# Splitting the last two plain fp32 weight units of an expert pair, with ScalarE and GpSimd

## The chip, the cores and the metric

One core of one Trainium2 chip runs the whole program. The metric is the device time of one execution in microseconds (us). A weight here is fp32; the kernel multiplies at fp32 accuracy by splitting a weight into a rounded part (type fp32r) and the rest, and adding two products.

## What is computed

One encoder layer over 16 meta tokens and 256 tokens of width 2048: a mixer (latent attention and retention), then a mixture of 32 experts in 4 groups, top 2 inside the top group. The change lies in the experts:

```python
def ffn(args):
    xb, e = args
    return (jax.nn.silu(xb @ w1[e]) * (xb @ w3[e])) @ w2[e]
```

w1 and w3 are 2048x512 for each expert, w2 is 512x2048, all float32: 12 MB an expert, 384 MB in all. Every expert's weights are read once a round.

## The kernel before, in words

**Units and pairs.** The mixer comes first (up to about 1163 us of the span). The experts' stage, from about 1206 us, goes over 16 pairs of experts (PAIRS). A pair has 24 weight units of 1 MB, [128 partitions x 2048] fp32, numbered x = 0 to 23: four each of w1, w3, w1 (the second expert), w2 (the first), w3 (the second), and w2 of the second, which is worked on four units into the next pair. A step k = x + 4 counts from there, so k = 0 is unit 20 of the pair before, and unit 22 is worked on at k = 2 of the next pair. Unit 10 is at k = 14.

**One unit's way.** SyncE loads it into one of 8 slots of raw2 (RING2), as soon as TensorE has finished unit x - 8. ScalarE rounds it into one of 4 slots of wh2 (`hi`, line 512), which it may do when TensorE has finished unit x - 4 (HELD). VectorE takes the difference, wl2 = raw2 - wh2, in place of raw2 (`lo`, line 623). TensorE (`unit`) multiplies with both: lines 869 and 870, four matmuls of 512 columns each, then counts the unit in s_used2. The profile names these tiles raw, wh and wl.

**The two plain units.** XR = (10, 22): these two units of a pair are neither rounded nor subtracted. TensorE reads raw2 as fp32 (line 866), in four matmuls that the profile records as eight passes.

**Order.** Each engine's program is written out by hand. In a step ScalarE first does copies that are due (L525: the finished products ab), then `hi(x + 4)`, then sigmoid (L529), the scaled output yall (L535) and the copies of gathered tokens (L517, at k = 4, 6, 8, 10, 16, 18, 20, 22). VectorE does `lo(x + 4)`, then `hidden` (L731 to L741, at k = 0 and 12), `output_rest` (L748, at k = 7 and 19) and `select` (L723, L724, at k = 9). TensorE does the unit, then `mix` (L891, L894, at k = 0 and 12: it waits for `select` and for the copies of ab), then the gathers (L850). GpSimd has only the scatters of finished rows (L479), one for each expert: parity 0 behind k = 19, parity 1 behind k = 7 of the next pair. The stage is one round here (the loop `more` is not entered).

```python
XR = (10, 22)
X_SPLIT = [sum(y not in XR for y in range(x)) for x in range(25)]
raw2 = place("raw2", [P, RING2, U], 0)
wl2 = place("wl2", [P, RING2, U], 0, F32R)
wh2 = place("wh2", [P, HELD, U], 65536, F32R)
```

Of the kernel before, what the change touches and what calls it, by code (L numbers as in the profile page):

```python
# [5 lines left out]
F32 = mybir.dt.float32  # L6
# [3 lines left out]
ALU = mybir.AluOpType  # L10
ACT = mybir.ActivationFunctionType
# [38 lines left out]
HELD = 4  # L50
# [41 lines left out]
def moe_trunk(nc, ins, out):  # L92
# [12 lines left out]
    def sem(name):  # L105
        return ctx.enter_context(nc.semaphore(name))

    with ctx:
# [50 lines left out]
        st = place("st", [P, 2, 3 * P], R0 + 6144)  # L159
# [113 lines left out]
        XR = (10, 22)  # L273
# [5 lines left out]
# [3 lines that stand above are left out]
# [49 lines left out]
        s_h1 = sem("s_h1")  # L331
# [12 lines left out]
        s_raw2 = [sem(f"s_raw2_{i}") for i in range(RING2)]  # L344
        s_wh2 = sem("s_wh2")
        s_wl2 = sem("s_wl2")
        s_used2 = sem("s_used2")
        s_ac = sem("s_ac")
        s_bc = sem("s_bc")
# [28 lines left out]
        def slot2(x):  # L378
            return (x + 4) % RING2

        def landed2(turn, x):

            return 16 * (24 // RING2 * turn + (x + 4) // RING2 + (slot2(x) >= 4))
# [90 lines left out]
        def pool_experts(pool):  # L474
            def scatter(filled, par):

                pool.wait_ge(s_h1, 1)
                pool.wait_ge(s_ye[par], filled)
                pool.indirect_dma_start(yscr[:, :], bass.IndirectOffsetOnAxis(dest[0:SLOTS, par:par + 1], 0),  # L479
                                        yall[0:SLOTS, par, :], None, bounds_check=SCRATCH_ROWS - 1,  # L480
                                        oob_is_err=False).then_inc(s_scat[par], 16)

            def pairs(first, end):
                with pool.Fori(first, end) as p:
                    scatter(p, 0)
                    scatter(p, 1)

            pairs(1, PAIRS + 1)
            pool.wait_ge(s_nx, 1)
            more = pool.value_load(nxi[0:1, 0:1], min_val=0, max_val=ROUNDS - 1)  # L490
            with pool.If(more > 0):
                pairs(PAIRS + 1, PAIRS * (more + 1) + 1)
            for par in range(2):
                pool.wait_ge(s_scat[par], 16 * PAIRS * (more + 1))
            nc.gpsimd.tensor_tensor(marks[:, 5:6], half[:, 0:1], half[:, 0:1], ALU.mult).then_inc(s_all, 1)

        def scalar_experts(act):

            act.wait_ge(s_wused, N_UNITS)
            for b in range(KD):  # L500
                act.wait_ge(s_h1t, b + 1)
                nc.scalar.activation(h1t[:, b, :], ps[:, b % 8, 0:SEQ], ACT.Copy).then_inc(s_h1tc, 1)

            def hi(turn, x):
                if x % 24 in XR:
                    return
                act.wait_ge(s_raw2[slot2(x)], landed2(turn, x))
                if isinstance(turn, int) and 24 * turn + x < HELD:
                    act.wait_ge(s_wused, N_UNITS)
                else:  # L510
                    done(act, turn, x - HELD)
                nc.scalar.activation(wh2[:, x % HELD, :], raw2[:, slot2(x), :], ACT.Copy).then_inc(s_wh2, 1)  # L512

            def gathered(g, par, q):

                act.wait_ge(s_gt, 8 * g + q + 1)
                nc.scalar.activation(xg[:, par, 2 * q:2 * q + 2, :, :],  # L517
                                     ps[:, 7 - q % 2, :].rearrange("p (k a c) -> p k a c", k=2, a=2),
                                     ACT.Copy).then_inc(s_xg, 1)

            def copy_up(turn, x, j, v):

                done(act, turn, x)
                need(act, s_hm, j)
                nc.scalar.activation(ab[:, v, :], ps[:, v, :], ACT.Copy).then_inc((s_ac, s_bc)[v], 1)  # L525

            def sigmoid(j):
                act.wait_ge(s_hm, j + 1)
                nc.scalar.activation(sg[:, :], ps[:, 6, 0:4 * SLOTS], ACT.Sigmoid).then_inc(s_sg, 1)  # L529

            def outputs(turn, x, j, par, before_):

                done(act, turn, x)
                need(act, s_scat[par], 16 * before_)
                nc.scalar.activation(yall[0:SLOTS, par, :].rearrange("p (b c) -> p b c", b=4), ps[0:SLOTS, 2:6, :],  # L535
                                     ACT.Copy, scale=wsc[0:SLOTS, par:par + 1]).then_inc(s_yc, 1)

            def pair(turn, par, first=False):
                for x in body(first):
                    k = step(x, first)  # L540
                    if k == 11:
                        copy_up(turn, x, 2 * turn, 1)
                    if k == 23:
                        copy_up(turn, x, 2 * turn + 1, 1)
                    hi(turn, x + HELD)
                    if k == 0 and not first:
                        sigmoid(2 * turn - 1)
                    if k == 3:
                        copy_up(turn, x, 2 * turn, 0)
                    if k == 7 and not first:  # L550
                        outputs(turn, x, 2 * turn - 1, 1, turn - 1)
                    if k == 12:
                        sigmoid(2 * turn)
                    if k == 15:
                        copy_up(turn, x, 2 * turn + 1, 0)
                    if k == 19:
                        outputs(turn, x, 2 * turn, 0, turn)
                    for q in range(8):
                        if k == (G_FIRST if first else G_AT)[q]:
                            gathered(turn + 1, 1 - par, q)  # L560

            def one_round(turn, ready=0):
                for x in range(ready, HELD):
                    hi(turn, x)
                pair(turn, 0, first=True)
                pair(turn + 1, 1)
                with act.Fori(1, PAIRS // 2) as i:
                    pair(turn + 2 * i, 0)
                    pair(turn + 2 * i + 1, 1)
                last = turn + PAIRS - 1  # L570
                sigmoid(2 * last + 1)
                outputs(last, 23, 2 * last + 1, 1, last)

            for x in range(HELD):
                hi(0, x)
            for n in range(2):
                act.wait_ge(s_r1, n + 1)
                dst = eg if n == 0 else ex
                nc.scalar.activation(dst[:, :, :], dst[:, :, :], ACT.Exp).then_inc(s_r2, 1)
            for q in range(8):  # L580
                gathered(0, 0, q)
            one_round(0, ready=HELD)
            act.wait_ge(s_nx, 1)
            more = act.value_load(nxi[0:1, 0:1], min_val=0, max_val=ROUNDS - 1)
            with act.If(more > 0):
                with act.Fori(0, more) as r:
                    one_round(PAIRS * (r + 1))
# [228 lines left out]
        def tensor_experts(pe):  # L816

            pe.wait_ge(s_h1, 1)
            for b in range(KD):
                need(pe, s_h1tc, b - 7)  # L820
                for t in range(TT):
                    m = nc.tensor.transpose(ps[:, b % 8, P * t:P * (t + 1)], mrg[:, t, P * b:P * (b + 1)], ident[:, :])
# [3 lines left out]
            for t in range(TT):  # L826
                for b in range(KD):
                    m = nc.tensor.matmul(ps[:, 6 + t, 0:N_GROUPS + N_EXP], h1t[:, b, P * t:P * (t + 1)], wr[:, b, :],
                                         start=b == 0, stop=b == KD - 1)
# [24 lines left out]

            def unit(turn, x, pairs_, start, stop):

                raw = x % 24 in XR
                if raw:
                    pe.wait_ge(s_raw2[slot2(x)], landed2(turn, x))
                else:  # L860
                    pe.wait_ge(s_wl2, split_units(turn, x) + 1)
                one = len({id(a[0]) for a in pairs_}) == 1
                for i, (o, s, c) in enumerate(pairs_):
                    st, sp_ = (start and (i == 0 or not one)), (stop and (i == 3 or not one))
                    if raw:
                        m = nc.tensor.matmul(o, s.bitcast(F32), raw2[:, slot2(x), c:c + 512], start=st, stop=sp_,  # L866
                                             skip_group_check=True)
                    else:
                        nc.tensor.matmul(o, s, wh2[:, x % HELD, c:c + 512], start=st, stop=False, skip_group_check=True)  # L869
                        m = nc.tensor.matmul(o, s, wl2[:, slot2(x), c:c + 512], start=False, stop=sp_,  # L870
                                             skip_group_check=True)
                m.then_inc(s_used2, 1)

            def up(turn, x, u, v, par, a):
# [1081 lines left out]
```

## Time and profile before

| | |
|---|---|
| median of 3 runs | 2248.09 us (2244.63 to 2248.26) |
| the profiled execution | 2248.71 us |
| its span | 2246.6 us |
| mean granted TensorE clock | 0.969 |
| busy: TensorE / VectorE / ScalarE / GpSimd | 2124.5 / 1573.4 / 1238.8 / 107.8 us |
| HBM read / written | 590.90 / 18.87 MB |

The profile is one execution. In its views each row is a group of instructions or a stretch of time; "busy" is the union of the times in which an engine worked, an arrow `<-` with a name behind it tells what ended an engine's idle time. Matmul ends are modelled, so the distance of two starts tells more than a matmul's length. PE is TensorE, PEld its weight load, DVE VectorE, ACT ScalarE, POOL GpSimd, SP SyncE.

### The profile page before, as it was taken

What the parts mean: (1) busy time and instruction counts of PE and PEld (TensorE: products, weight loads), DVE (VectorE), ACT (ScalarE), POOL (GpSimd) and SP (SyncE); (2) the same over time, 40 slices, a digit from 0 to 9 for tenths busy, and PEclk for the clock granted to TensorE, in tenths of its full rate; (3) what the DMA queues carried; (4) which work ended last, traced back from release to release, by engine and by line L of the source; (5) the groups of instructions that cost most, each with busy time, mean ns of one, the idle gap of its engine ahead of it and who ended that gap; (6) DMA issues with size and microseconds to landing.
All of it is one profiled execution on the core that took longest, in us unless ns stands there. A gap on an engine that the chain in (4) does not pass through costs nothing.

```text
span 2246.6 us, 30190 instructions
## 1 busy us (share of the span) xinstructions
PE 2124.5 (95%) x11513; PEld 1773.6 (79%) x11513; DVE 1573.4 (70%) x1348; ACT 1238.8 (55%) x1007; POOL 107.8 (5%) x76
## 2 busy tenths in 40 slices
PE   6999999999999999999978999999999999999991
PEld 5998777899998987887867777778777778777770
DVE  6545444453546365544466999989999999999986
ACT  3434443333232323333334888878887878888870
POOL 1000000000000000001000000000000000000001
PEclk9999999999999999999977999999999999999995
DMA  5554334655454544555544999999999999999973
GB/s 186 150 142 159 95 112 150 209 180 177 148 171 145 167 150 145 196 188 192 173 168 171 410 412 418 412 397 420 420 420 410 415 417 413 417 404 421 407 313 152
DMA packets 161974, 598.23 MB, mean 266 GB/s; under 512 B 20016, under 2 KB 28320, under 8 KB 110544
## 3 DMA queue, kind: packets, MB, share of 16 engines
q1 hardware_dynamic: 158224, 589.60, 69.2%
q0 software_dynamic: 3680, 7.64, 1.0%
q8 instruction: 50, 0.82, 0.1%
q14 instruction: 20, 0.16, 0.0%
HBM read 590.90 MB, written 18.87 MB: 271 GB/s over the span
## 4 chain that ended last, share of the span: by engine, by line
PE 74%; DVE 13%; issue 9%; ACT 2%; DMA 1%; POOL 1%; DVEq 0%; SPq 0%; POOLq 0%; ACTq 0%
PE ps L1551 20%; PE ps L1535 14%; PE ps L869 9%; DVE wl L623 9%; PE ps L870 9%; PE ps L866 5%; PE ps L850 3%; PE ps L891 3%; PE ps L1642 2%; PE ps L1622 2%; ACT wh L512 1%; PE ps L1609 1%; DVE yall L748 1%; PE ps L1663 1%; DMA yrow<-yscr 1%
## 5 line engine op out<-in xcount | busy, mean ns | idle before, releaser
L623 DVE TENSOR_TENSOR wl<-raw,wh 128x2048 fp32r<-128x2048 f32 x352 | 786.6, 2286 | 58.7 <-ACT wh L512 57.4
L512 ACT ACTIVATE wh<-raw 128x2048 fp32r<-128x2048 f32 x352 | 664.8, 1912 | 122.2 <-PE ps L870 71.9
L1198 DVE TENSOR_TENSOR wl<-raw,wh 128x2048 fp32r<-128x2048 f32 (+1 forms) x169 | 382.2, 2264 | 310.2 <-ACT wh L1031 310.2
L1031 ACT ACTIVATE wh<-raw 128x2048 fp32r<-128x2048 f32 (+1 forms) x169 | 319.9, 1896 | 463.4 <-DMA raw<-in_w_in_dram 283.6
L869 PE MATMUL ps<-wh,xg 128*128 128x512 f32 x900 | 382.4, 425 | 0.8 <-issue 0.7
L870 PE MATMUL ps<-wl,xg 128*128 128x512 f32 x900 | 359.4, 399 | 0.0
L1535 PE MATMUL ps<-hth,wh 128*128 128x272 f32 (+1 forms) x896 | 260.0, 290 | 5.0 <-DVE wl L1198 3.6
L1535 PE MATMUL ps<-htl,wh 128*128 128x272 f32 (+1 forms) x896 | 256.9, 287 | 0.0
L1535 PE MATMUL ps<-hth,wl 128*128 128x272 f32 (+1 forms) x896 | 256.8, 287 | 0.0
L869 PEld LDWEIGHTS ps<-wh,xg 128*128 128x128 f32 x900 | 173.4, 193 | 52.4 <-DVE wl L623 9.7
L869 PE MATMUL ps<-wh,hx 128*128 128x512 f32 x508 | 204.6, 403 | 3.4 <-DVE hx L741 3.4
L870 PEld LDWEIGHTS ps<-wl,xg 128*128 128x128 f32 x900 | 173.6, 193 | 40.6 <-issue 7.4
L870 PE MATMUL ps<-wl,hx 128*128 128x512 f32 x508 | 200.1, 394 | 0.0
L1535 PEld LDWEIGHTS ps<-hth,wh 128*128 128x128 f32 x896 | 169.5, 189 | 8.0 <-issue 3.5
L1535 PEld LDWEIGHTS ps<-htl,wh 128*128 128x128 f32 x896 | 169.4, 189 | 0.3
L1535 PEld LDWEIGHTS ps<-hth,wl 128*128 128x128 f32 x896 | 169.1, 189 | 0.0
L1551 PE MATMUL ps<-wh,hth 128*128 128x512 f32 x384 | 154.6, 403 | 0.0
L1551 PE MATMUL ps<-wh,htl 128*128 128x512 f32 x384 | 151.0, 393 | 0.0
L1551 PE MATMUL ps<-wl,hth 128*128 128x512 f32 x384 | 150.9, 393 | 0.0
L479 POOL DMA_INDIRECT yscr<-yall,dest x32 | 73.3, 2292 | 980.1 <-DVE yall L748 980.1
L869 PEld LDWEIGHTS ps<-wh,hx 128*128 128x128 f32 x508 | 96.4, 190 | 23.1 <-DVE hx L741 3.5
L866 PE MATMUL ps<-raw,xg 128*128 128x512 f32 x248 | 113.3, 600 | 0.0
(315 smaller groups left out, 3105.0 us busy)
## 6 DMA issues: line engine op xcount, KB each, us to landing
raw<-in_w_dram SPq DMA_DIRECT2D x384, 1024.0 KB, 8.1
raw<-in_w_in_dram SPq DMA_DIRECT2D x104, 1024.0 KB, 5.1
raw<-in_w_pa_dram SPq DMA_DIRECT2D x16, 1024.0 KB, 5.1
raw<-in_w_pb_dram SPq DMA_DIRECT2D x16, 1024.0 KB, 5.1
raw<-in_w_out_dram SPq DMA_DIRECT2D x16, 1024.0 KB, 5.1
raw<-in_w_ukv_dram SPq DMA_DIRECT2D x8, 1024.0 KB, 5.4
yrow<-yscr SPq DMA_DIRECT2D x4, 1024.0 KB, 9.8
raw<-in_w_uq_dram SPq DMA_DIRECT2D x8, 384.0 KB, 3.6
```

Of the source, the lines that this page charges most:

```text
L479: pool.indirect_dma_start(yscr[:, :], bass.IndirectOffsetOnAxis(dest[0:SLOTS, par:par + 1], 0), yall[0:SLOTS, par, :], None, bounds_check= ...
L512: nc.scalar.activation(wh2[:, x % HELD, :], raw2[:, slot2(x), :], ACT.Copy).then_inc(s_wh2, 1)
L623: nc.vector.tensor_tensor(wl2[:, slot2(x), :], raw2[:, slot2(x), :], wh2[:, x % HELD, :].bitcast(F32), ALU.subtract).then_inc(s_wl2, 1)
L850: m = nc.tensor.matmul(bank[:, b, :, h, :], src[:, t, 2 * q + b, :], pg[:, t, :].rearrange("p (a s) -> p a s", a=2), start=t == 0, stop=t ...
L866: m = nc.tensor.matmul(o, s.bitcast(F32), raw2[:, slot2(x), c:c + 512], start=st, stop=sp_, skip_group_check=True)
L869: nc.tensor.matmul(o, s, wh2[:, x % HELD, c:c + 512], start=st, stop=False, skip_group_check=True)
L870: m = nc.tensor.matmul(o, s, wl2[:, slot2(x), c:c + 512], start=False, stop=sp_, skip_group_check=True)
L891: nc.tensor.matmul(ps[:, 6, c:c + SLOTS], ab[:, v, P * f:P * (f + 1)], fold[:, :], start=True, stop=True, skip_group_check=True)
L1031: nc.scalar.activation(wh[:, n % RING1, 0:c], raw1[:, n % RING1, 0:c], ACT.Copy).then_inc(s_wh, 1)
L1198: nc.vector.tensor_tensor(wl[:, n % RING1, 0:c], raw1[:, n % RING1, 0:c], wh[:, n % RING1, 0:c].bitcast(F32), ALU.subtract).then_inc(s_wl, 1)
L1535: m = nc.tensor.matmul(ps[:, bank, col:col + width], w[:, n % RING1, c:c + P], s[:, 4 * u + k, c0:c0 + width], start=opens and u == 0 and ...
L1551: m = nc.tensor.matmul(ps[:, bank + t, :], s[:, 4 * u + k, c:c + P], w[:, n % RING1, 512 * k:512 * (k + 1)], start=u == 0 and k == 0 and j ...
```

## The change

Units 10 and 22 go the same way as the others up to the difference. ScalarE rounds them too, in their turn of the order. Their difference is made by GpSimd (`residue`), in place over raw2, ahead of the scatter of the same parity. Two semaphores each (s_hx for rounded, s_lx for subtracted) take the place of s_wh2 and s_wl2 for these units, so that the counts of the other 22 stay. TensorE waits for s_lx in place of the load, and has one form of unit. VectorE's program is unchanged.

```diff
+        s_hx = [sem(f"s_hx{i}") for i in range(len(XR))]
+        s_lx = [sem(f"s_lx{i}") for i in range(len(XR))]
...
+            def residue(filled, i):
+
+                x = XR[i]
+                pool.wait_ge(s_h1, 1)
+                pool.wait_ge(s_hx[i], filled)
+                nc.gpsimd.tensor_tensor(wl2[:, slot2(x), :], raw2[:, slot2(x), :], wh2[:, x % HELD, :].bitcast(F32),
+                                        ALU.subtract).then_inc(s_lx[i], 1)
+
             def pairs(first, end):
                 with pool.Fori(first, end) as p:
+                    residue(p, 0)
                     scatter(p, 0)
+                    residue(p, 1)
                     scatter(p, 1)
...
             def hi(turn, x):
-                if x % 24 in XR:
-                    return
+                made = s_hx[XR.index(x % 24)] if x % 24 in XR else s_wh2
...
-                nc.scalar.activation(wh2[:, x % HELD, :], raw2[:, slot2(x), :], ACT.Copy).then_inc(s_wh2, 1)
+                nc.scalar.activation(wh2[:, x % HELD, :], raw2[:, slot2(x), :], ACT.Copy).then_inc(made, 1)
...
             def unit(turn, x, pairs_, start, stop):
 
-                raw = x % 24 in XR
-                if raw:
-                    pe.wait_ge(s_raw2[slot2(x)], landed2(turn, x))
+                if x % 24 in XR:
+                    pe.wait_ge(s_lx[XR.index(x % 24)], turn + x // 24 + 1)
...
-                    if raw:
-                        m = nc.tensor.matmul(o, s.bitcast(F32), raw2[:, slot2(x), c:c + 512], start=st, stop=sp_,
-                                             skip_group_check=True)
-                    else:
-                        nc.tensor.matmul(o, s, wh2[:, x % HELD, c:c + 512], start=st, stop=False, skip_group_check=True)
-                        m = nc.tensor.matmul(o, s, wl2[:, slot2(x), c:c + 512], start=False, stop=sp_,
-                                             skip_group_check=True)
+                    nc.tensor.matmul(o, s, wh2[:, x % HELD, c:c + 512], start=st, stop=False, skip_group_check=True)
+                    m = nc.tensor.matmul(o, s, wl2[:, slot2(x), c:c + 512], start=False, stop=sp_,
+                                         skip_group_check=True)
```

## Rows read from the trace of the kernel before

**Rows 1.** The page: GB/s that the DMA engines moved, span in 40 slices.
```profile
GB/s 186 150 142 159 95 112 150 209 180 177 148 171 145 167 150 145 196 188 192 173 168 171 410 412 418 412 397 420 420 420 410 415 417 413 417 404 421 407 313 152
```

**Rows 2.** Timeline of GpSimd: start, duration, instruction, idle time before and who ended it.
```profile
1255.11 2.27 POOL L479 DMA_INDIRECT yscr<-yall,dest  x1 [103.53 <-DVE yall L748]
...
1654.91 2.26 POOL L479 DMA_INDIRECT yscr<-yall,dest  x1 [27.44 <-DVE yall L748]
1685.79 2.25 POOL L479 DMA_INDIRECT yscr<-yall,dest  x1 [28.63 <-DVE yall L748]
...
2176.85 2.25 POOL L479 DMA_INDIRECT yscr<-yall,dest  x1 [28.63 <-DVE yall L748]
```

**Rows 3.** Two pairs: PE, PEld, DVE, ACT, POOL busy; clock, DMA share, GB/s.
```profile
1625.22:1685.79 60.57, 59.61 (x297) 47.45 (x297) 57.90 (x40) 50.93 (x39) 4.50 (x3) 1.00 1.01 421
1685.79:1747.99 62.20, 61.22 (x297) 48.71 (x297) 57.89 (x40) 50.91 (x39) 4.50 (x2) 0.97 1.01 412
```

**Rows 4.** The same view, at a fall of the granted clock in another pair.
```profile
1415.00:1420.00 5.00, 5.00 (x12) 3.13 (x12) 3.12 (x8) 1.97 (x2) 0.00 (x0) 0.67 1.01 410
```

**Rows 5.** Pair from 1625.22: tile raw (idle until, landing), then the DMA view.
```profile
  ACT wh L512: 2.3, 4
...
DMA to landing us min/median/max: 6.5/8.2/10.2
...
GB/s 411 427 427 427 417 417 427 422 417 422 427 433 417 411 433 411 422 422 427 433 406 422 433 422 417 422 417 433 400 417 406 417 411 422 422 411 433 422 433 422
DMA packets 3615, 25.50 MB, mean 421 GB/s; under 512 B 503, under 2 KB 503, under 8 KB 503
```

**Rows 6.** Groups by line from 1400 to 2100 us: busy, mean ns, idle before.
```profile
L623 DVE TENSOR_TENSOR wl<-raw,wh 128x2048 fp32r<-128x2048 f32 x251 | 560.8, 2286 | 39.6 <-ACT wh L512 38.8
L512 ACT ACTIVATE wh<-raw 128x2048 fp32r<-128x2048 f32 x250 | 472.2, 1912 | 89.5 <-PE ps L870 52.4 <-PE ps L866 36.5 <-DMA raw<-in_w_dram 0.5
```

**Rows 7.** Waits from 1400 to 2100 us: us in total, times, longest.
```profile
PE ps L891 <- DVE wdc L724: 11.6, 12, 1.0
```

**Rows 8.** Timeline of TensorE: mix, a plain unit (x = 10), a split one; unit 22 last.
```profile
1659.51 1.99 PE L891 MATMUL ps<-fold,ab 128*128 128x64 f32 x16 [0.96 <-DVE wdc L724]
...
1663.67 3.59 PE L866 MATMUL ps<-raw,xg 128*128 128x512 f32 x8
1666.70 0.79 PE L869 MATMUL ps<-wh,xg 128*128 128x512 f32 x1
1667.33 0.40 PE L870 MATMUL ps<-wl,xg 128*128 128x512 f32 x1
1667.56 0.39 PE L869 MATMUL ps<-wh,xg 128*128 128x512 f32 x1
...
1693.37 3.60 PE L866 MATMUL ps<-raw,xg 128*128 128x512 f32 x8
```

**Rows 9.** Timeline of ScalarE around unit 10, and the roundings before unit 22.
```profile
1653.37 1.91 ACT L512 ACTIVATE wh<-raw 128x2048 fp32r<-128x2048 f32 x1
1656.58 0.60 ACT L525 ACTIVATE ab<-ps 128x512 f32<-128x512 f32 x1 [0.82 <-PE ps L870]
1657.07 3.70 ACT L512 ACTIVATE wh<-raw 128x2048 fp32r<-128x2048 f32 x2
...
1663.87 1.91 ACT L512 ACTIVATE wh<-raw 128x2048 fp32r<-128x2048 f32 x1 [1.54 <-PE ps L870]
...
1684.23 1.91 ACT L512 ACTIVATE wh<-raw 128x2048 fp32r<-128x2048 f32 x1
```

**Rows 10.** Groups by line: the smallest tensor_tensor of GpSimd and of VectorE.
```profile
L495 POOL TENSOR_TENSOR marks<-half 128x1 f32<-128x1 f32 x1 | 0.4, 408 | 2.3 <-DMA yscr<-yall,dest 2.3
...
L735 DVE TENSOR_TENSOR dest<-ps,beyond 128x1 uint32<-128x1 f32 x32 | 4.7, 148 | 0.0
```

**Rows 11.** Timeline of VectorE around the mix of 1659.51.
```profile
1654.10 4.49 DVE L623 TENSOR_TENSOR wl<-raw,wh 128x2048 fp32r<-128x2048 f32 x2
1658.52 0.68 DVE L723 TENSOR_TENSOR pd<-slots,rk__144 128x512 f32<-128x512 f32 x1
```

## The prediction, made before the changed kernel had run

> **What bounds the kernel now.** I read the page first. The slices [rows 1] show the experts' stage from about 1206 us on: the DMA engines move 400 to 420 GB/s there, twice what they do before it. The 16 pairs of experts repeat, and GpSimd's scatters mark them [rows 2]: one scatter of each pair starts at 1255.11 us and the same one of the last pair at 2176.85 us, 15 pairs in 921.7 us, so 61.45 us a pair. The pairs are of two kinds. The one from 1625.22 takes 60.57 us at a granted clock of 1.00, the next takes 62.20 us at 0.97 [rows 3]. In the slow kind TensorE ran for a while at the lower of its levels, 1.2 instead of 2.4 GHz; such a fall lies at 1415 to 1420 us too, with a mean of 0.67 and TensorE busy all the time [rows 4].
>
> None of three resources is idle enough to be set aside, as the busy times of the clean pair show. In its 60.57 us TensorE (PE) is busy 59.61 us, VectorE (DVE) 57.90 us, so that it is idle 2.67 us; ScalarE (ACT) is busy 50.93 us, GpSimd (POOL) 4.50 us, and the DMA engines report a share of 1.01 [rows 3]. A load lands 8.2 us after its issue (median) while 24 of them share 60.57 us, one each 2.52 us, so three are in flight all the time, at 421 GB/s [rows 5]. The waits say the rest: ScalarE waits for TensorE to free a slot of wh (52.4 and 36.5 us in 700 us), VectorE for ScalarE (38.8 us), hardly anybody for a DMA (0.5 us) [rows 6], and TensorE waits now and then for VectorE, 12 times for the select alone [rows 7]. So two resources are nearly used up, VectorE with 2.67 us to spare in a pair and the DMA engines with about nothing, and TensorE's order of work ties them together.
>
> **What the change removes.** On TensorE a plain unit is eight passes: the next unit starts 3.03 us after the first pass at 1663.67, and its second product 0.63 us later, where 0.23 us is the usual step, so the unit occupies 3.03 + 0.40 = 3.43 us [rows 8]. A split unit is eight matmuls 0.23 us apart (1667.33 to 1667.56), 1.84 us. Two units a pair: 2 x 1.6 = 3.2 us of TensorE's time go. That alone buys little. The waits of ScalarE for L866 (36.5 us in the 700 us, or 3.2 us a pair) and part of VectorE's for L512 go with it, but what is late next is the DMA: it moves 25.50 MB a pair at 421 GB/s [rows 5], and its best slices are 427 to 433. At 427 GB/s a pair would be 59.7 us. So the most that the removal can give is 61.45 - 60.57 = 0.9 us a pair if only the slow kind of pair goes, or 1.75 us if the DMA also reaches 427: 14 to 28 us over 16 pairs.
>
> **What it adds on ScalarE.** Two roundings a pair at 1.91 us [rows 6], 3.8 us; busy time goes from 50.93 to 54.7 us of 60.57. They fall into the holes: hi(10) would start at 1655.2, when the rounding of 1653.37 ends, and end at 1657.1; a copy of gathered tokens and the one of 1656.58, half a microsecond each, then come before the roundings of 1657.07, which start at about 1658.0, 0.9 us late. ScalarE has 1.54 us idle ahead of 1663.87 to make it good [rows 9]. VectorE's difference of 1659.19 starts perhaps 0.7 us late. I cost it at nothing, covered by such idle time at each of the two places; without that cover it is up to 0.9 us a place, 1.8 us a pair, 29 us in all.
>
> **What it adds on GpSimd.** Two tensor_tensor of 128x2048 fp32 a pair, in place over raw. No row shows GpSimd reading a tile of that size. From below I bound it by the same form on VectorE, 2286 ns [rows 6]. From above: on the smallest form (128x1) GpSimd takes 408 ns and VectorE 148 ns [rows 10], 2.76 times, and 2.76 x 2.286 = 6.3 us. That factor is mostly fixed cost, the lower end assumes an engine built for such work; I take the middle, D = 4.3 us. The Trainium skill, "GPSIMD Engine Reference", section 3.1, gives 4497 ns for a GpSimd tensor_tensor add of 2048 fp32 elements; no run here shows it, and with it the sum below would end at 2342 us.
>
> Does TensorE wait for it? For x = 10, hi(10) ends at 1657.1 and TensorE wants the unit at 1663.67: 6.5 us of cover. For x = 22, GpSimd is free from its scatter at 1688.04, hi(22) ends at about 1688.0 (behind the rounding of 1684.23, ahead of the gathered copy), and TensorE wants it at 1693.37: 5.3 us of cover [rows 2, 8, 9]. With D = 4.3 both fit. In GpSimd's queue the scatter of parity 0 stands behind residue(10), which is over 24 us before it is due, and the scatter of parity 1 behind residue(22), due some 22 us later. GpSimd idles 27 to 29 us between scatters [rows 2], so nobody waits there.
>
> **What it does to VectorE** decides. Both engines then read whole tiles of raw and wh and write wl at the same time, VectorE without a pause. No row shows the two together on tiles. The nearest is the scatter at 1654.91, 2.26 us long, beside the two differences of 1654.10, which still take 4.49 us together [rows 2, 11]; but there GpSimd writes descriptors and reads no tile. So the loss s of VectorE per residue lies between 0 and D (a gain is excluded: VectorE's instructions are the same in number and size). VectorE has no queue to spare: a pair would take the larger of 60.57 us and 57.90 + 2s + 0.37 us, where 0.37 is the idle time of a clean pair that isn't a wait for L512 (2.67 - 2.3) [rows 3, 5]. That passes today's 61.45 us at s = 1.6 us. Of the interval from 0 to 4.3 us, 63% lies above that. I take the upper end, s = D: two differences on VectorE itself never overlap (1654.10: two in 4.49 us [rows 11]), and an instruction of the same kind, on the same two tiles, that must go through the same memory counts for me as if it stood in that queue, at its longer duration. The place can be seen: residue(10) would take over at 1658.5, between the second difference and the select of L723 [rows 11]; the select, the mix of 1659.51 behind it [rows 8] and all later differences move back by D. The Trainium skill, "SBUF — State Buffer", section "Who interferes with whom", says that a VectorE instruction with two SBUF inputs and a GpSimd instruction that reads SBUF exclude each other, and that the later one blocks for the whole of the earlier. It speaks against this change; no row here shows it, and by it s is D less what falls beside VectorE's PSUM forms.
>
> **The sum.** 57.90 + 2 x 4.3 + 0.37 = 66.9 us a pair against 61.45: +5.4 us, 16 pairs: +87 us. The profiled execution took 2248.7 us (its span of 2246.6 and 2.1 around it), 0.6 us above the median of the three runs, so I add to it: 2248.7 + 87 = 2335 us. With D = 2.29 it is +1.4 a pair, 2272 us; with D = 6.3 it is +9.4, 2400 us. TensorE saves 3.2 us a pair that nobody needs, and the DMA engines fall to 25.50 / 66.9 = 381 GB/s.
>
> **Rivals.**
> A. No interference (s near 0), faster. For it: the untouched 4.49 us beside the scatter. Then VectorE has its 2.67 us, the plain units' delay is gone, the pairs of 62.20 us become 60.57 or less, and the DMA ends it: 2248.7 - 14 = 2235 us, down to 2220 if 427 GB/s hold. It decides up to s = 1.15 us ((60.57 - 58.27) / 2). Against it: TensorE would stand idle oftener, and the falls of its clock may go on.
> B. Partial interference, s from 1.15 to 3 us: 60.6 to 64.3 us a pair, 2235 to 2294 us. For it: GpSimd needs more time per element than VectorE, so it can't use the memory all the time.
> C. GpSimd slower than its cover without harming VectorE: at D = 6.3 the x = 22 unit is 1.0 us late (6.3 - 5.3), and ScalarE's 1.8 us come on top: 16 x 2.8 = +45 less the 14 gained, 2280 us at the most, about 2250 if only one of them acts. Against it: TensorE is ahead of the other two elsewhere.
> D. The units aren't cheaper on TensorE, that is, the change doesn't do what it says. It would matter in A only (2249 us); the rows of all other split units speak against it.
>
> **How the numbers follow.** The forecast (s = D, 2300 to 2400 us) has 0.50, A 0.24, B 0.18, C and D 0.08. Within 0.2% of before (about what a measurement of this kernel can tell from no change, here 2244 to 2253 us) lie the part of B with s from 1.45 to 1.75 us (0.03) and half of C and D (0.04), together 0.07. Faster are A and the part of B with s under 1.45 us, 0.27; the rest, 0.66, is slower. The range starts at 2233 us, which takes in the main value of A, and ends at 2365 us, D = 5.2 us (57.90 + 10.4 + 0.37 = 68.7, 16 x 7.2 = 116); above and below it I leave 0.15. The slow cases' own range is 2270 to 2365.
>
> **What would show it.** After: scatters 66 to 67 us apart; VectorE busy over 95% of the stage, or its difference at L623 no longer 2.28 us at all times but some of 6 us; no more waits of ScalarE for TensorE; TensorE waiting for VectorE (L869 behind wl, L891 behind wdc); 380 GB/s. A GpSimd row with the duration D, 32 times. I am wrong if all differences still take 2.28 us and no hole of GpSimd's length stands between them: then s is near 0 and rival A holds, with the scatters at 60.6 us.

## The result and the profile after

| | before | after |
|---|---|---|
| median | 2247.29 us (4 runs beside the changed kernel) | 2406.68 us (4 runs, 2402.92 to 2407.36) |
| ratio, 95% interval | | 1.0699 (1.0687 to 1.0712) |
| the profiled execution, its span | 2248.71, 2246.6 us | 2402.92, 2400.9 us |
| mean granted TensorE clock | 0.969 | 0.94 |

The kernel is 7.0% slower, 159 us or 9.9 us a pair. The direction is the forecast one. The time is 72 us above the predicted 2335 us and 42 us above the range's end.

Line numbers have moved: L623 is L634, L723 and L724 are L734 and L735, L891 is L897, L869 and L870 are L875 and L876, L512 is L523, L479 is L481, and the new residue is L490. Two pairs, scatter to scatter, as in [rows 3] (PE, PEld, DVE, ACT, POOL busy; clock, DMA share, GB/s):

```profile
1616.46:1688.06 71.60, 61.95 (x298) 51.33 (x297) 65.14 (x40) 54.67 (x41) 16.09 (x4) 0.90 0.88 354
1688.06:1759.74 71.68, 61.94 (x298) 51.40 (x297) 65.14 (x40) 54.71 (x41) 16.07 (x5) 0.90 0.89 357
```

Over 15 pairs the mean is 71.30 us, against 61.45 [rows 2]. VectorE's busy time grew by 7.24 us [rows 3], though its program is unchanged. But it is idle 6.46 us as well. The clock is 0.90 to 0.93 in every pair (0.95 to 1.00 before), and the DMA engines are no longer full.

GpSimd and VectorE around unit 10 and around unit 22 show what is shut out. VectorE before is in [rows 11]. Timeline of GpSimd:

```profile
1651.89 5.77 POOL L490 TENSOR_TENSOR wl<-raw,wh 128x2048 fp32r<-128x2048 f32 x1
1688.06 2.25 POOL L481 DMA_INDIRECT yscr<-yall,dest  x1 [30.41 <-DVE yall L759]
1690.38 5.79 POOL L490 TENSOR_TENSOR wl<-raw,wh 128x2048 fp32r<-128x2048 f32 x1
```

Timeline of VectorE, the same stretches:

```profile
1648.80 4.49 DVE L634 TENSOR_TENSOR wl<-raw,wh 128x2048 fp32r<-128x2048 f32 x2
1653.21 5.00 DVE L734 TENSOR_TENSOR pd<-slots,rk__144 128x512 f32<-128x512 f32 x1
1658.13 0.16 DVE L735 COPY wdc<-wd 128x8 f32 x1
...
1687.25 4.49 DVE L634 TENSOR_TENSOR wl<-raw,wh 128x2048 fp32r<-128x2048 f32 x2
1693.03 7.49 DVE L634 TENSOR_TENSOR wl<-raw,wh 128x2048 fp32r<-128x2048 f32 x2 [1.29 <-ACT wh L523]
```

GpSimd's first difference starts at 1651.89, while VectorE works until 1653.29, and ends at 1657.66. The select then takes 5.00 us instead of 0.68 [rows 11]: 4.3 us shut out. At unit 22 two differences take 7.49 instead of 4.49 us: 3.0 us. GpSimd waits too: from 1691.74, where VectorE's two differences end, to its own end at 1696.17 are 4.4 us of its 5.79.

Now TensorE, which waits for that select. Timeline of TensorE behind the mix of k = 12; before, that mix started 0.96 us late and the next unit 2.25 us after it (1659.51 to 1661.76):

```profile
1652.88 0.39 PE L876 MATMUL ps<-wl,xg 128*128 128x512 f32 x1
1658.52 3.67 PE L897 MATMUL ps<-fold,ab 128*128 128x64 f32 x16 [5.26 <-DVE wdc L735]
1661.98 0.96 PE L900 MATMUL ps<-wdc,pd 128*128 128x2 f32 x4
1662.80 0.77 PE L875 MATMUL ps<-wh,xg 128*128 128x512 f32 x1
...
1668.07 0.63 PE L875 MATMUL ps<-wh,xg 128*128 128x512 f32 x1
1668.50 0.58 PE L876 MATMUL ps<-wl,xg 128*128 128x512 f32 x1
1668.91 0.39 PE L875 MATMUL ps<-wh,xg 128*128 128x512 f32 x1
1669.15 0.39 PE L876 MATMUL ps<-wl,xg 128*128 128x512 f32 x1
```

The same in stretches of 3 us, with the columns of the two pairs above:

```profile
1652.00:1655.00 3.00, 1.26 (x6) 0.70 (x4) 3.00 (x2) 3.00 (x2) 3.00 (x1) 1.00 1.01 421
1655.00:1658.00 3.00, 0.00 (x0) 0.00 (x0) 3.00 (x1) 0.21 (x1) 2.65 (x1) 0.54 1.03 429
1658.00:1661.00 3.00, 2.48 (x12) 2.48 (x12) 3.00 (x4) 0.00 (x0) 0.00 (x0) 0.50 0.42 178
1661.00:1664.00 3.00, 3.00 (x13) 2.81 (x13) 2.29 (x5) 0.38 (x1) 0.00 (x0) 0.50 0.00 0
1664.00:1667.00 3.00, 3.00 (x9) 2.32 (x8) 1.00 (x3) 0.40 (x1) 0.00 (x0) 0.50 0.00 0
```

TensorE stands idle 5.26 us, its granted clock falls to 0.50, which is 1.2 GHz, during that time, and it stays there until about 1668.9. The matmuls start 0.43 instead of 0.23 us apart. The mix now takes 4.28 us to the next unit's start, 2.0 more, and the 6.1 us from 1662.80 to 1668.91 hold 14 matmuls that need 3.2 us at the full clock: 4.9 us lost in all. In that stretch everybody else runs dry: VectorE has nothing to subtract (1.00 of 3 us busy), ScalarE nothing to round, the loads stop (0 GB/s).

The pairs differ in one thing. From the second pair on the wait before this mix is 5.2 to 5.3 us, but the stretch at the lower clock behind it lasts 7.0 to 10.4 us. One pair of each kind (the mix of the second starts at 1945.11, and the matmuls are 0.23 us apart again from 1952.10):

```profile
1831.39:1903.05 71.66, 62.03 (x298) 51.40 (x297) 65.14 (x40) 54.68 (x41) 16.07 (x5) 0.90 0.88 352
1903.05:1973.51 70.46, 60.79 (x299) 50.56 (x299) 65.06 (x40) 54.93 (x42) 16.10 (x4) 0.93 0.89 360
```

With 3.4 us less at the lower clock the pair is 1.2 us shorter. On a straight line 10.4 us of it would cost 3.7 us a pair. That is an estimate from pairs that all have a fall; no run has this wait without one.

### The profile page after: what moved, and what is told of

It is laid out like the page before. It is cut to its first block, busy times and chain, and to the rows that moved or that the text cites. A ratio compares the mean times of both kernels' runs of the same rounds, so it can differ in the third digit from the quotient of the medians.

```text
span 2400.9 us, 30290 instructions
## 1 busy us (share of the span) xinstructions
PE 2140.6 (89%) x11513; PEld 1820.8 (76%) x11513; DVE 1690.5 (70%) x1348; ACT 1296.8 (54%) x1039; POOL 292.2 (12%) x108
## 3 DMA queue, kind: packets, MB, share of 16 engines
q1 hardware_dynamic: 158224, 589.60, 65.6%
## 4 chain that ended last, share of the span: by engine, by line
PE 61%; issue 18%; DVE 8%; ACT 7%; DMA 4%; POOL 1%; DVEq 0%; SPq 0%; ACTq 0%; POOLq 0%
PE ps L1557 18%; PE ps L1541 13%; PE ps L875 7%; PE ps L876 7%; ACT wh L523 5%; DVE wl L634 4%; DMA raw<-in_w_dram 3%; PE ps L861 2%; PE ps L897 2%; PE ps L1648 1%; PE ps L1628 1%; PE ps L1615 1%; ACT xg L528 1%; PE ps L1669 1%; DMA yrow<-yscr 1%
## 5 line engine op out<-in xcount | busy, mean ns | idle before, releaser
L634 DVE TENSOR_TENSOR wl<-raw,wh 128x2048 fp32r<-128x2048 f32 x352 | 835.7, 2427 | 87.0 <-ACT wh L523 85.6
L523 ACT ACTIVATE wh<-raw 128x2048 fp32r<-128x2048 f32 x384 | 723.6, 1914 | 138.1 <-PE ps L876 136.4
L875 PE MATMUL ps<-wh,xg 128*128 128x512 f32 x1024 | 436.2, 426 | 36.4 <-ACT xg L528 18.9
L876 PE MATMUL ps<-wl,xg 128*128 128x512 f32 x1024 | 423.0, 413 | 0.0
L875 PEld LDWEIGHTS ps<-wh,xg 128*128 128x128 f32 x1024 | 208.4, 203 | 94.2 <-issue 24.6
L876 PEld LDWEIGHTS ps<-wl,xg 128*128 128x128 f32 x1024 | 207.1, 202 | 42.8
L875 PE MATMUL ps<-wh,hx 128*128 128x512 f32 x512 | 206.7, 404 | 30.5 <-DVE hx L752 30.5
L876 PE MATMUL ps<-wl,hx 128*128 128x512 f32 x512 | 201.3, 393 | 0.0
L490 POOL TENSOR_TENSOR wl<-raw,wh 128x2048 fp32r<-128x2048 f32 x32 | 184.4, 5763 | 73.5 <-ACT wh L523 72.5
L481 POOL DMA_INDIRECT yscr<-yall,dest x32 | 73.3, 2292 | 872.9 <-DVE yall L759 872.9
L897 PE MATMUL ps<-fold,ab 128*128 128x64 f32 x512 | 87.7, 344 | 84.0 <-DVE wdc L735 82.4
L897 PEld LDWEIGHTS ps<-fold,ab 128*128 128x128 f32 x512 | 85.4, 257 | 92.3 <-issue 91.1
```

What stands on the lines that cost most here:

```text
L490: nc.gpsimd.tensor_tensor(wl2[:, slot2(x), :], raw2[:, slot2(x), :], wh2[:, x % HELD, :].bitcast(F32), ALU.subtract).then_inc(s_lx[i], 1)
L634: nc.vector.tensor_tensor(wl2[:, slot2(x), :], raw2[:, slot2(x), :], wh2[:, x % HELD, :].bitcast(F32), ALU.subtract).then_inc(s_wl2, 1)
L897: nc.tensor.matmul(ps[:, 6, c:c + SLOTS], ab[:, v, P * f:P * (f + 1)], fold[:, :], start=True, stop=True, skip_group_check=True)
```

## The experiments

Two things had to be told apart. Theory 1: GpSimd's long reading instruction shuts VectorE out, and TensorE's wait behind the shut-out select lets its clock fall, which costs again. The rival: the split units themselves, by two more roundings on ScalarE or by TensorE idling oftener. The quoted paragraphs say what was expected before each run. All ratios are against the kernel before, run on the same chip.

**GpSimd's work nearly gone.**

```diff
-                nc.gpsimd.tensor_tensor(wl2[:, slot2(x), :], raw2[:, slot2(x), :], wh2[:, x % HELD, :].bitcast(F32),
+                nc.gpsimd.tensor_tensor(raw2[:, slot2(x), 0:64], raw2[:, slot2(x), 0:64], wh2[:, x % HELD, 0:64].bitcast(F32),
...
-                    m = nc.tensor.matmul(o, s, wl2[:, slot2(x), c:c + 512], start=False, stop=sp_,
-                                         skip_group_check=True)
+                    w_ = wh2[:, x % HELD, c:c + 512] if x % 24 in XR else wl2[:, slot2(x), c:c + 512]
+                    m = nc.tensor.matmul(o, s, w_, start=False, stop=sp_, skip_group_check=True)
```

> The changed kernel, but GpSimd subtracts only the first 64 of 2048 columns of units 10 and 22, and TensorE multiplies these two units twice with the rounded part (the same eight matmuls), so the small part of their weights is left out of the result. Roundings on ScalarE, waits and matmul counts stay. Theory 1 (GpSimd's long instruction shuts VectorE out, and TensorE's wait for the select that follows drops its clock): nothing is shut out, the select of VectorE takes 0.68 us again, pairs take 60.6 us or a little less, 2225 to 2243 us. Rival (the split units themselves, by ScalarE's two roundings or by TensorE idling more, cost the time): still over 2350 us.

Measured: 2237.26 us, 0.9947 (0.9930 to 0.9963), 60.76 us a pair. The rival falls: with both units split and rounded, and GpSimd's work nearly gone, the kernel is 0.5% faster than before (12 us). All of the 159 us, and some 10 more, hang on GpSimd's long instruction. The select takes 0.81 us here instead of 0.68, and the mix still waits 1.1 us. The pairs with a clock of 1.00 take 59.9 to 60.8 us, those with less up to 61.8.

**The two differences on VectorE.**

```diff
-        XR = (10, 22)
+        XR = ()
```

(in the kernel before)

> The kernel before with all 24 units split, the differences of units 10 and 22 made by VectorE, GpSimd unchanged. Theory 1: VectorE's 57.9 us a pair grow by 2 x 2.22 to 62.3, with 0.4 idle 62.7 us a pair, 2248.7 + 16 x 1.25 = 2269 us, far below the 2407 of the changed kernel. Rival (the split units themselves cost the time): over 2350 us here too.

Measured: 2259.39 us, 1.0047 (1.0030 to 1.0064), 62.27 us a pair, each within 0.1 us. VectorE is busy 696.32 of 700 us. It is bound as its sum says (62.3 us busy, 0.3 idle; the time is 10 us under the 2269 that I expected), and doing this work itself costs 10 us, where handing it to GpSimd costs 159. The mix of k = 12 still waits 0.96 us here, and the clock falls in about one pair of four: that wait doesn't always bring a fall.

**One unit each.** Unit 22 alone, then unit 10 alone; the other stays plain. The edit drops one residue and gives its unit the load's wait and the fp32 matmul back:

```diff
+        PLAIN = (10,)
...
-                    residue(p, 0)
                     scatter(p, 0)
                     residue(p, 1)
```

> The changed kernel for unit 22 alone; unit 10 stays plain fp32 as before. Theory 1: unit 22 shuts out 3.0 us of VectorE that no mix waits for directly; VectorE needs 57.9 + 3.0 + 0.4 = 61.3 us a pair, so 2245 to 2265 us. If both units cost alike: 2248 + 80 = about 2328 us.

Measured: 2301.27 us, 1.0242 (1.0223 to 1.0261), 64.78 us a pair, well above what I expected. VectorE's busy time (656.56 of 700 us) is as computed, 61 us a pair. But it is idle 4 us a pair: its idle time lies at other places and doesn't take up what is lost at unit 22. The pairs are of two kinds, 64.05 us at a clock of 1.00 and 65.63 us at 0.97, where the kernel before has 60.57 and 62.20. So unit 22 costs 3.5 us a pair where the clock doesn't fall at all. Two more waits of TensorE stand there, both 10 times in 700 us:

```profile
PE ps L884 <- DVE hx L754: 16.0, 10, 1.6
PE ps L884 <- ACT xg L530: 12.5, 10, 1.3
```

The first is the shut-out passed on through hidden; the second is the rounding of unit 22, which stands in ScalarE's order ahead of the last gathered copy, for which the next pair's first unit waits.

> The changed kernel for unit 10 alone; unit 22 stays plain fp32 as before. Unit 22 alone cost 52 us (2301 against 2249). Theory 1: unit 10 has the longer shut-out (4.3 us) in front of the mix and the fall of the clock, so the larger part: 159 - 52 = about 107 us, 2350 to 2362 us, with TensorE's clock at 1.2 GHz behind the mix of k = 12 and nowhere else. If the two share the loss in proportion to the shut-out alone (4.3 to 3.0): 52 x 4.3 / 3.0 = 75 us, 2324 us.

Measured: 2348.74 us, 1.0449 (1.0432 to 1.0467), 67.71 us a pair, with a mean clock of 0.92 between 1400 and 2100 us, where the run with unit 22 alone has 0.99. That is just under the 2350 to 2362 us that I expected. Unit 10 costs 101 us, unit 22 52 us, together 153 of the 159. Split by the shut-out alone, unit 10 would have cost 75.

**The select out of harm's way.** Two steps. First k = 8 in place of 9 in the changed kernel:

```diff
-                    if k == 9:
+                    if k == 8:
                         select(turn, p)
```

> The changed kernel, with VectorE's select one step earlier (k = 8 instead of 9), so that it stands ahead of GpSimd's instruction for unit 10 and TensorE's mix doesn't wait for it. Theory 1: a difference of VectorE is shut out in its place, for the same 4.3 us; TensorE's wait before the mix and the fall of its clock are gone or shorter; pairs near VectorE's own sum of 65.1 + 0.4 us, 2248.7 + 16 x 4.1 = about 2315 us. If the shut-out alone makes the whole loss and the clock nothing: unchanged, 2400 us.

Measured: 2355.31 us, 1.0470 (1.0453 to 1.0488), 68.34 us a pair: 51 us won, where I expected 92, for a reason that the timeline of VectorE shows:

```profile
1635.11 0.68 DVE L734 TENSOR_TENSOR pd<-slots,rk__144 128x512 f32<-128x512 f32 x1
1635.71 4.87 DVE L735 COPY wdc<-wd 128x8 f32 x1
```

The select got through, and the copy of eight columns behind it was shut out in its place (4.87 instead of 0.16 us). The mix needs that too and still waited, 3.5 us a pair. The group of GpSimd's instruction has a mean of 5219 ns in this run, for the one at unit 10 didn't start under a long instruction of VectorE and takes 4.55 us:

```profile
1635.98 4.55 POOL L490 TENSOR_TENSOR wl<-raw,wh 128x2048 fp32r<-128x2048 f32 x1
```

That is D itself. Then three steps earlier:

```diff
-                    if k == 9:
+                    if k == (8 if first else 6):
                         select(turn, p)
```

> The changed kernel, with VectorE's select moved to k = 6, three steps earlier (k = 8 in the first pair, which has no steps 4 to 7). The run with k = 8 left the copy of wdc behind the select shut out for 4.7 us and the mix waiting for it; now both are done long before. Theory 1: TensorE's wait before the mix and the fall of the clock behind it go; VectorE is still shut out 4.3 and 3.0 us a pair. Between VectorE's own sum (65.6 us a pair, 2315 us) and the pair of the run without long GpSimd work plus the full 7.3 us (60.7 + 7.3 = 68.0 us, 2353 us), nearer to the first. If the clock costs nothing: as the changed kernel less the 0.8 us by which TensorE's wait shrinks, 2390 us.

Measured: 2332.95 us, 1.0379 (1.0362 to 1.0397). One pair of it:

```profile
1624.31:1690.94 66.63, 59.23 (x296) 48.43 (x296) 66.30 (x40) 54.94 (x41) 16.17 (x5) 0.97 0.98 383
```

VectorE is busy 66.30 of 66.63 us in this pair. Two differences of it are shut out, 4.3 to 4.4 us each (four in a row take 13.26 instead of 8.90 us). That is so in 4 of the 15 pairs. In most of the others one of the two shut-outs is 3.0 us and VectorE is busy 65.0 and idle 1.6 us, at the same length of the pair. So VectorE is held up no less than in the changed kernel, and yet the kernel is 74 us faster, 4.4 us a pair (71.30 to 66.86). The wait before the mix isn't in the list of waits any more, and the clock is 0.97 over the 700 us. So about half of the loss is the wait before the mix with the fall of the clock, and about half is VectorE's lost time. No run parts the wait from the fall; the estimate of 3.7 us a pair from the pairs of the changed kernel would give the fall most of the 4.4.

**Does reading or length matter?** GpSimd writes a whole tile and reads none:

```diff
-                nc.gpsimd.tensor_tensor(wl2[:, slot2(x), :], raw2[:, slot2(x), :], wh2[:, x % HELD, :].bitcast(F32),
-                                        ALU.subtract).then_inc(s_lx[i], 1)
+                nc.gpsimd.memset(raw2[:, slot2(x), :], 0.0).then_inc(s_lx[i], 1)
```

(and the matmuls as in the first experiment)

> The changed kernel, but GpSimd writes zeros over the raw tile of units 10 and 22 (128x2048 fp32, nothing read) in place of the difference, and TensorE multiplies these two units twice with the rounded part, so their small part is left out of the result. If what shuts VectorE out is GpSimd's reading: no difference or select of VectorE is longer than before, 2225 to 2245 us, whatever the length of the memset up to 5 us. If it is any GpSimd access: the instruction beside it is longer by the memset's length, and the time lies above 2290 us. A plain copy of VectorE may be held in either case.

Measured: 2237.00 us, 0.9956 (0.9939 to 0.9973). The tile wl on VectorE, from 1400 to 2100 us (min/median/max):

```profile
L633 DVE TENSOR_TENSOR wl<-raw,wh x254: 2281/2286/2294, 1399.5 to 2098.8; 128x2048 fp32r<-128x2048 f32 x127
```

and one memset with what VectorE did beside it:

```profile
1650.20 1.82 POOL L490 MEMSET raw<- 128x2048 f32 x1
...
1649.29 2.28 DVE L633 TENSOR_TENSOR wl<-raw,wh 128x2048 fp32r<-128x2048 f32 x1
1651.49 0.69 DVE L733 TENSOR_TENSOR pd<-slots,rk__144 128x512 f32<-128x512 f32 x1
```

None of 254 differences is longer; in the changed kernel the longest took 5720 ns. The select that starts under this memset takes 0.69 us, but the memset has only 0.5 us left then. The first pair shows more (GpSimd, then VectorE):

```profile
1225.86 1.81 POOL L490 MEMSET raw<- 128x2048 f32 x1 [73.87 <-ACT wh L522]
...
1226.16 0.69 DVE L733 TENSOR_TENSOR pd<-slots,rk__144 128x512 f32<-128x512 f32 x1
1226.77 0.94 DVE L734 COPY wdc<-wd 128x8 f32<-128x8 f32 x1
```

The whole select lies inside the memset and takes 0.69 us. The copy behind it starts inside the memset too and ends 0.04 us after it: 0.94 us instead of 0.16. So a memset does hold up a VectorE copy, and not a VectorE instruction that reads two tiles. GpSimd's memset (1.82 us) is shorter than its difference (4.55 us), so no run has a long GpSimd instruction that only writes.

**In four pieces.**

```diff
+                for c in range(4):
+                    s = nc.gpsimd.tensor_tensor(wl2[:, slot2(x), 512 * c:512 * (c + 1)], raw2[:, slot2(x), 512 * c:512 * (c + 1)],
+                                                wh2[:, x % HELD, 512 * c:512 * (c + 1)].bitcast(F32), ALU.subtract)
+                s.then_inc(s_lx[i], 1)
```

> The changed kernel with each difference of GpSimd in four instructions of 512 columns. If GpSimd and VectorE take turns instruction by instruction: no VectorE instruction is longer than before by more than about 1.4 us, the select is done some 3 us sooner and TensorE's clock mostly holds, but one residue lasts four GpSimd pieces and three VectorE differences, about 4.6 + 6.6 = 11 us, and TensorE waits for unit 10 or 22 itself: 2300 to 2360 us. If GpSimd keeps the way between its pieces: as the changed kernel, 2400 us.

Measured: 2403.12 us, 1.0691 (1.0673 to 1.0709). My time is wrong, the mechanism is there. GpSimd and VectorE take turns. Timeline of GpSimd (the row at 1616.42 is unit 22's, the one at 1652.19 unit 10's), then of VectorE:

```profile
1616.42 10.35 POOL L491 TENSOR_TENSOR wl<-raw,wh 128x512 fp32r<-128x512 f32 x4
...
1652.19 10.79 POOL L491 TENSOR_TENSOR wl<-raw,wh 128x512 fp32r<-128x512 f32 x4
```

```profile
1653.46 1.76 DVE L736 TENSOR_TENSOR pd<-slots,rk__144 128x512 f32<-128x512 f32 x1
1655.14 1.23 DVE L737 COPY wdc<-wd 128x8 f32 x1
1656.29 5.55 DVE L636 TENSOR_TENSOR wl<-raw,wh 128x2048 fp32r<-128x2048 f32 x2
```

The select, the copy and one of the two differences each wait 1.1 us for one piece, and one residue lasts 10.4 to 10.8 us. The mix still waits 3.1 us for wdc, and TensorE waits 3.6 us a pair for the residue of unit 22 itself; the mean clock is 0.88 between 1400 and 2100 us. What VectorE won TensorE lost. The expectation that the clock would mostly hold failed with it.

**What the kernel before can gain.** It has the same weak place in small, 0.96 us of wait before the mix [rows 8]. The select at k = 6 (8 in the first pair) in the kernel before, nothing else:

> The kernel before with VectorE's select at k = 6 (k = 8 in the first pair) in place of 9, nothing else. There TensorE waited about 1 us for the select in every pair, and in about half of them its clock fell behind that mix (62.2 instead of 60.57 us). Theory 1 (a wait in front of the mix lets the clock fall): the slow kind of pair goes, all take 60.6 us, 2228 to 2240 us. Rival (the falls of the kernel before have another cause): no change, 2244 to 2252 us.

Measured: 2238.63 us, 0.9953 (0.9940 to 0.9967). The pairs are 60.2 to 61.1 us, mean 60.76; none of 62.2 is left and the clock is 1.00 from 1400 to 2100 us:

```profile
1400.00:2100.00 700.00, 684.99 (x3406) 546.67 (x3405) 670.05 (x450) 593.94 (x439) 51.84 (x23) 1.00 1.01 418
```

This is the best kernel here that computes everything, 7% under the changed one's time. Its mean pair is as long as that of the run with GpSimd's work nearly gone (60.76 us). ScalarE now waits 54.6 us in 700 for loads, where it was 0.5 before, so the DMA engines are the next limit. Whether split units would gain anything beside the early select isn't tested: the run with GpSimd's work nearly gone still has the wait of 1.1 us and falls of the clock, and its pairs without a fall are as short as 59.9 us.

With unit 22 split besides, its difference on VectorE (`XR = (10,)`):

> The kernel before with select at k = 6 and only unit 10 plain; unit 22 is split, with its difference on VectorE and nothing on GpSimd. By VectorE's sum: 57.9 + 2.2 + 0.4 = 60.5 us a pair, as much as a pair with both plain takes, so 2230 to 2240 us, no gain over the run with the earlier select alone. If idle time of VectorE in the order of its work isn't filled by the added difference: 2.2 us more a pair, 2270 us.

Measured: 2248.78 us, 1.0001 (0.9992 to 1.0010), 61.34 us for most pairs. In between: 0.8 us a pair more than the expected 60.5 and 0.6 more than with both units plain, with TensorE waiting for the gathered copy (13.7 us in 700) behind the rounding of unit 22 again. So VectorE's sum isn't fully reached, nor the added 2.2 us fully paid.

## Why the prediction was right or wrong

**Right: the mechanism.** The select at 1653.21 is shut out by residue(10), and the mix and what follows moves back: that is the place that was named. The shut-out is total for the rest of GpSimd's instruction, s near D (4.3 us at unit 10). The Trainium skill, "SBUF — State Buffer", "Who interferes with whom", states it for a GpSimd instruction that reads, and not for one that only writes; here 5.00 us for the select beside GpSimd's difference and 0.69 us inside its memset agree with both halves. D was taken as 4.3 us from two far bounds; it is 4.55 us. The 4497 ns of the Trainium skill ("GPSIMD Engine Reference", 3.1) agree with the trace within 0.1 us.

**The sum, in another kernel.** "57.90 + 2s + 0.37" with s = 4.3 gave 66.9 us a pair and 2335 us. With the select at k = 6, where the wait before the mix is gone, 66.86 us and 2332.95 us were measured. In 4 of its 15 pairs the terms agree too (0.33 us idle); in the others a smaller shut-out and more idle time come to the same length, which is luck. In the changed kernel the two shut-outs are 4.3 and 3.0 us, so the sum would have been 57.90 + 7.3 + 0.37 = 65.6 us, against 71.30 measured.

**Wrong: the step that took a pair as the larger of two sums.** The prediction moved "the mix of 1659.51 behind it" back by D and charged nothing for what TensorE does while it stands. VectorE isn't bound there: 6.46 us idle where 0.37 were allowed. The missing term at unit 10 is TensorE's wait of 5.26 us, in which the clock falls to 1.2 GHz, and up to 10.4 us of work at that level (1658.52 to 1668.91). Between the changed kernel and the one with the select at k = 6 it makes 4.4 us a pair, as much as the forecast was short (71.30 against 66.9). That these agree so well is partly luck: the second shut-out was 3.0 and not 4.3 us, which should have made the pair 1.3 us shorter, and VectorE's idle time took that back. The same step fails at unit 22 without any fall of the clock: alone it takes 64.78 us a pair, where the sum with s = 3.0 is 61.3, for VectorE's shut-out reaches TensorE through hidden while VectorE's idle time stands elsewhere. The cause was in sight: the pairs of 60.57 and 62.20 us [rows 3, 4], read as two kinds of pair, and used only for the gain. The right use was as a price: in the kernel before a wait of 0.96 us at the same mix brought 1.6 us in half of the pairs.

Of the signs that the prediction named, a GpSimd row near D, a longer select and the wait at the mix came. Three came out otherwise: VectorE is busy 91% of the 700 us and not over 95, ScalarE still waits 85.4 us in 700 for TensorE where no such wait was expected, and the scatters are 71.3 us apart and not 66 to 67. All three say that VectorE alone isn't the bound.

**ScalarE at nothing** was nearly right at unit 10 and not at unit 22. There the rounding stands ahead of the gathered copy, and TensorE waits 1.3 us a pair for it, 12.7 us in 700. With GpSimd's work nearly gone this wait is there as well (17.2 us in 700), and the kernel is still 12 us faster than before. What the wait alone costs isn't measured.

**The cover of 5.3 us at unit 22** held: no wait of TensorE for L490 is in the list of the changed kernel. TensorE waits for a residue only in other kernels: up to 0.45 us, at either unit, with the select at k = 6, and 3.6 us at unit 22 in pieces.

**The DMA** fell to 354 GB/s, not 381, in step with the longer pair. **Rival A's** price was right too: without interference 2237 us were measured, where 2235 were given. It didn't happen because GpSimd reads. **The range** ended at D = 5.2 us; it covered a longer GpSimd instruction but not a second effect of the first one.

## What to carry to other kernels

Work that was taken off a busy VectorE and given to GpSimd stayed on VectorE's bill at GpSimd's longer duration, where both read tiles of SBUF: 2.2 us of work became 3.0 to 4.4 us of shut-out, and the same work on VectorE itself cost 10 us instead of 159. When an instruction can be held up, look for who waits behind it, and move the short one that TensorE waits for (here the select) far ahead of it; a wait of TensorE is to be priced at its length and at the slow clock that may follow. Before adding an engine to a stage, look at whether a small wait already lets the clock fall: moving one small instruction by three steps gave 11 us, about as much as the split gave with GpSimd's work nearly gone (12 us).

## What wasn't expected of the hardware

- A VectorE copy of 128x8 elements is shut out like a big instruction: 4.87 us instead of 0.16.
- GpSimd is held up by VectorE as well: 5.8 us when VectorE was at work at its start, 4.55 us when it wasn't.
- The two take turns between instructions: with four GpSimd pieces, each VectorE instruction that came between two of them waited about 1.1 us.
- A GpSimd memset of 128x2048 fp32 takes 1.82 us. It holds up no VectorE difference and no select, but once a copy of 128x8: 0.94 us instead of 0.16.
- The granted clock was at 0.50 behind a wait of 5.2 to 5.3 us in every pair of the changed kernel from the second on, and TensorE's next 7.0 to 10.4 us of work ran at that level. Behind a wait of 0.96 us in the kernel before it fell in about half of the pairs.
